# Eight modulation products move from TensorE to VectorE, and the expert ring gets a seventh buffer

## The chip, the cores and the metric

The kernel runs on one core of a Trainium2 chip. The metric is the device time of one execution in microseconds (us). It was measured three times; the median is 1368.77 us. A separate, profiled execution gives the trace that is read below.

## The reference

A two-part transformer block in float32, 256 tokens of width 1024. The change touches the modulation vectors of the first part and the buffers of its experts. Cut to what matters:

```python
# _adaln: one row vector c, silu, times w_mod (1024 x 6144), plus b_mod; six chunks of 1024
sh1, sc1, g1, sh2, sc2, g2 = split(silu(c) @ w_mod + b_mod, 6)
hc = rmsnorm(ctx, norm1_g) * (1 + csc1) + csh1      # csc1, csh1: the same with c_ctx
hx = rmsnorm(x,   norm1_g) * (1 + sc1)  + sh1
# w_in (1024 x 5664) gives u, q, k, v, g, gates and the low-rank decays; for ctx only k, v, decays
ox = gla_bidirectional(qx, kx, vx, ...)             # 4 heads, chunks of 64
x  = x + g1 * mixer_out(pooled, ox, ...)
x  = x + g2 * hier_moe(rmsnorm(x, norm2_g) * (1 + sc2) + sh2, ...)
# hier_moe: 32 experts, each w1, w3 (1024 x 512) and w2 (512 x 1024); top 2 of one group per token
# then two layers (attention + MLP) and four layer norms: second_block
```

w_mod is read as 12 slabs of 1024 x 512. Slabs 0 to 3 (sh1, sc1) are needed at once, for x and for ctx. Slabs 4 to 11 (g1, sh2, sc2, g2) are needed only for x, at the end of the mixer and later.

## The kernel before

**Stages.** The mixer (to about 332 us of the trace), the experts (to about 773 us), two layers (to the end). All weights are read in slabs of 2 MB by DMAs that SP issues in one order (`slab_plan`), each into one of eleven slots of SBUF. The issue waits until the slab that was in the slot before (`BEFORE`) has been used (`slab_freed`). SP works through its queue in order, so a load that waits holds all later ones.

**Each engine's order is written out by hand.** PSUM is used as a ring of four banks; `bank_plan` lists every use in order, with the engine (V or A) that empties it. A use of a bank by TensorE waits until the use four places earlier has been emptied. Behind each other in TensorE's queue in the mixer stand: keys, ctx keys, `v` 0 and 1 (values of x, first half), `cum`, `remc` (decays), `v` 2 and 3 (ctx), `qT`, `v` 4 and 5, `v` 6 and 7, then four heads (`states`, `crossings`, `read_out`), `u`, `g` and the rest of the mixer, which is one long run of matmuls. A w_in slab is split into a high part (ScalarE, `pre_hi`, the tile `prehi`) and a low part (VectorE, `pre_lo`, `prelo`), in two halves, and each `v` or `qT` product waits for the low parts.

**Modulation slabs 4 to 11, before.** `mod_rows(s)` on TensorE multiplies the 32-column tile `scol` (silu of c, 8 tiles of 128 rows) with the slab: eight matmuls, four at a time in four 32-column groups of the array, which leave four partial rows in a bank. ScalarE copies them (`mod_hi`), VectorE takes the rest (`mod_low`, `mod_lo`), and `mod_bc(s)` adds the four rows and spreads the sum to all partitions by two matmuls with the constant `row_pick`. VectorE's `mod_bc(s)` adds the result to the bias rows. All eight slabs but one use slot 2, one after the other. The w_in slabs share the slots 0, 1 and 2 with them. Slot 10 (the tile `own`) is free, and takes slab 2 of the experts early, at the load of modulation slab 6.

**Experts.** Experts are worked on one after the other, four to a turn: an up product (w1 and w3), a down product (w2), and the scatter into the accumulator. Slabs 0 to 10 of the 96 (three for each expert) go into eleven slots (`AHEAD_SLOTS`) as the mixer frees them. Slabs 11 to 95 go around six slots (`MOE_SLOTS`); slot 0 is not used again until the first layer's first slab.

Of the kernel before, what the change touches and what calls it, by code (L numbers as in the profile page):

```python
# [7 lines left out]
P = 128  # L8
D = 1024
KT = D // P  # L10
# [4 lines left out]
NH = 4  # L15
# [95 lines left out]
EXPERTS_PER_TURN = 4  # L111
# [7 lines left out]
MODS = (0, 2, 1, 3)  # L119
MIXER_SLOT = {("mod", 0): 2, ("mod", 2): 1, ("mod", 1): 6, ("mod", 3): 2, ("w_in", 2): 0, ("w_in", 3): 1, ("w_in", 1): 0,  # L120
              ("w_in", 4): 1, ("w_in", 0): 0, ("w_in", 5): 1, ("w_in", 6): 2, ("w_in", 7): 0, ("w_in", 8): 1, ("w_in", 9): 2,
              ("w_in", 10): 0, ("pool_br", 0): 1, ("gla_br", 0): 2, ("gla_br", 1): 0, ("w_o", 0): 1, ("w_o", 1): 2}
# [19 lines left out]
def bank_plan():  # L142
# [7 lines left out]
    order += [("mod_rows", 4, "V"), ("v", 0, "A"), ("v", 1, "A")]  # L150
    order += [("cum", i, "A") for i in range(4)]
    order += [("remc", i, "A") for i in range(4)]
    order += [("mod_bc", 4, "V"), ("mod_rows", 5, "V"), ("v", 2, "A"), ("v", 3, "A"), ("mod_bc", 5, "V"), ("qT", 0, "V"), ("qT", 1, "V")]
    order += [("mod_rows", 6, "V"), ("v", 4, "A"), ("v", 5, "A"), ("mod_bc", 6, "V"), ("mod_rows", 7, "V"), ("v", 6, "A"), ("v", 7, "A")]
    order += [("mod_bc", 7, "V"), ("mod_rows", 8, "V")]
    for h in range(NH + 1):
        if h < NH:
            order += [("s0", h, "A"), ("sT", (h, 0), "V"), ("sT", (h, 1), "V")]
        if h == 0:
            order += [("mod_bc", 8, "V")]  # L160
        else:
            order += [("o", h - 1, "A")] + [("mod_bc", h + 7, "V")] * (h > 1) + [("mod_rows", h + 8, "V")] * (h < NH)
    order += [("u", 0, "A"), ("u", 1, "A")] + [("g", (0, j), "V") for j in range(2)]
# [21 lines left out]
OWN_SLOT = 10  # L185
AHEAD_SLOTS = (3, 6, OWN_SLOT, 1, 5, 2, 4, 7, 8, 0, 9)
MOE_SLOTS = (OWN_SLOT, 3, 6, 5, 1, 2)
# [6 lines left out]
for _n, (_name, _s) in enumerate(SLABS):  # L194

    if _name == "moe":
        _slot = AHEAD_SLOTS[_s] if _s < AHEAD else MOE_SLOTS[(_s - AHEAD) % len(MOE_SLOTS)]
# [44 lines left out]
def build(nc, a, out):  # L242
# [8 lines left out]
    with ctx:  # L251
# [69 lines left out]
        mod_hi, mod_lo = (split_at(f"mod_{what}", 44 * K1 + 512 * i, 512) for i, what in enumerate(("hi", "lo")))  # L321
# [83 lines left out]
        row_pick = ctx.enter_context(nc.sbuf_tensor("row_pick", [P, P], F32R))  # L405
# [67 lines left out]
        names = "x1_ready modhi_ready row_pick_ready tmp_ready base_ready ssq_ready lstd_ready centred_sum ht_ready hid_ready hlow_ready hsq_ready hhi_ready hlo_ready chi_ready clo_ready prehi_ready prelo_ready pre_used kT_done kc_done kT_ready ghi_ready glo_ready yhi_ready ylo_ready mlow_ready gated mixed zhi_ready zlo_ready abs_ready L_ready lr_ones whi_ready split_ready xhi_ready xlo_ready atthi_ready chosen_ready flag_ready pick_ready put_ready dcol_ready dsilu_scaled scol_zero scol_ready square_ready nstd_ready tn_ready mod_ready c_ready exp1_ready lr_part keys_ready cross_ready h_ready ez_ready ostd_ready on_ready z_ready lg_diff rexp_ready comb_ready ssq_half out_stored eps_ready ttok_ready gain_ready s1_ready hidT_ready put_done projected rope_read rot_ready value_ready scored masked max_ready exp_ready turned_done pT_ready weighted_done att_ready share_diff share_exp scaled_ready crossed_done attlo_ready".split()  # L473
# [149 lines left out]
        def slab_freed(n):  # L623
# [10 lines left out]
            if name == "w_in":  # L634
                bank_use = {0: ("u", 1), 1: ("qT", 1), 3: ("v", 3), 4: ("v", 7)}[s]
            else:
                bank_use = ("mod_rows", s)
# [33 lines left out]
        def _(sp):  # L671
# [31 lines left out]
            moe0, per, ring_ = SLAB_AT["moe", 0], 12, len(MOE_SLOTS)  # L703
            looped = AHEAD + ring_
# [4 lines left out]
            for (name, s), n in SLAB_AT.items():  # L709
# [14 lines left out]
                if (name, s) == ("w_in", 9):  # L724
                    load_expert(moe0, 0, 0)
                    spread(bc_n2, a["norm2_g"][0], bc2_in)
                    sp.dma_start(xres, a["x"][0].rearrange("(a p) n -> p a n", p=P)).then_inc(x_again, 16)
                if (name, s) == ("w_o", 1):
# [19 lines left out]
                elif 3 <= s < looped or s >= looped + per * (TURNS - 2):  # L748
                    s = {3: 9, 5: 3, 6: 5, 8: 6, 9: 10, 10: 8, 11: 12, 12: 11}.get(s, s)
# [16 lines left out]
                elif s == looped:  # L766
                    def loads_of_turn(it):
                        for j in range(looped, looped + per):
                            what, before = slab_freed(moe0 + j - ring_)
# [26 lines left out]
        def _(act):  # L796
# [26 lines left out]
            def mod_rows(s):  # L823
                b = take("mod_rows", s)
                if s in MODS:
                    act.activation(mod_slot(s), b, ACT.Copy).then_inc(freed["A"], 1)
                else:
                    act.activation(mod_hi, b, ACT.Copy).then_inc(G["modhi_ready"], 1)
# [93 lines left out]
            mod_rows(4)  # L922
# [12 lines left out]
            mod_rows(5)  # L935
# [5 lines left out]
            mod_rows(6)  # L941
# [3 lines left out]
            mod_rows(7)  # L945
# [4 lines left out]
            mod_rows(8)  # L950
# [7 lines left out]
            for h in range(NH):  # L958
# [5 lines left out]
                if h + 1 < NH:  # L964
                    mod_rows(h + 9)
# [292 lines left out]
        def _(dve):  # L1258
# [52 lines left out]
            def mod_low(s):  # L1311

                b = bank_of("mod_rows", s)
                dve.wait_ge(G["modhi_ready"], s - 3)
# [1452 lines left out]
```

## Time and profile before

| what | value |
|---|---|
| median of 3 runs | 1368.77 us (1365.86 to 1369.69) |
| profiled execution, its own time | 1368.02 us |
| its span in the trace | 1366.2 us |
| TensorE busy | 1198.1 us, 88% of the span |
| VectorE busy | 651.6 us, 48% |
| ScalarE busy | 485.2 us, 36% |
| DMA | 371.95 MB, mean 272 GB/s |
| chain that ended last | PE 69%, DMA 23%, DVE 3%, ACT 2% |

The profile page gives shares over the whole span. This kernel has three stages with different limits, so the windows by stage say more than the page: they give, for a stretch of time, how long each engine was busy, the granted TensorE clock and the DMA rate. The chain that ended last tells what each stretch waited for. The timeline gives single instructions with the idle time before them in square brackets. PE is TensorE, PEld its weight loads, DVE is VectorE, ACT is ScalarE, SPq the queue of SP. An fp32 matmul stands in the trace as two instructions.

### The profile page before, as it was taken

The numbers are of one execution on the slowest core, as the hardware profiler recorded it, in microseconds if no ns is written. First come the engines' busy times: TensorE is split into PE (matmuls) and PEld (weight loads), VectorE is DVE, ScalarE is ACT, GpSimd is POOL, SyncE is SP. The second block draws the span as 40 slices with busy tenths as digits, with TensorE's granted clock in tenths as the row PEclk, the third lists the DMA queues.
The fourth block names the chain that finished last, engine by engine and source line by source line (L and its number), as shares of the span: only waits on it lengthen the run. The fifth ranks groups of instructions, "written<-read, shape, count | busy, mean of one in ns | idle before, by whom it ended". The sixth has DMA issues, their size and how long they took to land.

```text
span 1366.2 us, 22173 instructions
## 1 busy us (share of the span) xinstructions
PE 1198.1 (88%) x9435; PEld 921.6 (67%) x9435; DVE 651.6 (48%) x991; ACT 485.2 (36%) x695; POOL 0.2 (0%) x4
## 2 busy tenths in 40 slices
PE   5999999999866666766766899999999999999997
PEld 4677788887434233433433599878888799888886
DVE  4445446786121010210101377576666767766665
ACT  5552346555101000000000346454444456554443
POOL 0000000000000000000000000000000000000000
PEclk9999999999998887888987999999999999999999
DMA  9677666579999999999999972436364444554620
GB/s 343 257 254 239 223 227 247 198 279 385 412 375 427 427 428 428 426 427 429 428 428 427 397 260 98 150 123 246 134 237 151 175 155 154 185 203 166 223 86 31
DMA packets 89115, 371.95 MB, mean 272 GB/s; under 512 B 6490, under 2 KB 8328, under 8 KB 76364
## 3 DMA queue, kind: packets, MB, share of 16 engines
q1 hardware_dynamic: 87480, 369.73, 69.1%
q10 hardware_dynamic: 1556, 1.08, 0.3%
q8 instruction: 61, 1.00, 0.3%
q14 instruction: 18, 0.15, 0.0%
HBM read 369.74 MB, written 1.05 MB: 271 GB/s over the span
## 4 chain that ended last, share of the span: by engine, by line
PE 69%; DMA 23%; DVE 3%; ACT 2%; issue 1%; SPq 1%; ACTq 0%; DVEq 0%
DMA arena<-in_moe_w 20%; PE ring L2038 8%; PE ring L2482 7%; PE ring L2027 5%; PE acc L2130 4%; PE acc L2131 4%; PE acc L2132 4%; PE ring L2040 4%; PE ring L2029 2%; DMA arena<-in_w_mod 2%; PE acc L2011 2%; PE acc L2013 2%; PE acc L2012 2%; PE ring L2176 1%; PE ring L2178 1%; PE ring L2177 1%
## 5 line engine op out<-in xcount | busy, mean ns | idle before, releaser
L2482 PE MATMUL ring<-arena 128*32 128x256 f32 x2048 | 153.6, 466 | 73.9 <-DMA arena<-in_moe_w 73.9
L2482 PEld LDWEIGHTS ring<-arena 128*32 128x32 f32 x2048 | 76.4, 133 | 146.5 <-DMA arena<-in_moe_w 69.4
L1284 DVE TENSOR_TENSOR wlo<-arena,whi 128x2048 fp32r<-128x2048 f32 x56 | 128.0, 2290 | 49.9 <-ACT whi L843 49.9
L1708 DVE TENSOR_TENSOR arena<-arena,ring 128x128 f32<-128x128 f32 x32 | 12.1, 379 | 257.7 <-ACT arena L1088 257.7
L1088 ACT ACTIVATE arena<-ring 128x128 f32<-128x128 f32 x32 | 8.9, 277 | 349.1 <-PE ring L2482 349.1
L843 ACT ACTIVATE whi<-arena 128x2048 fp32r<-128x2048 f32 x56 | 106.8, 1910 | 42.2 <-PE acc L2132 25.4
L2038 PE MATMUL ring<-xboth,whi 128*128 128x512 f32 x320 | 113.8, 398 | 0.0
L2040 PE MATMUL ring<-xboth,wlo 128*128 128x256 f32 x320 | 89.8, 281 | 0.0
L2038 PEld LDWEIGHTS ring<-xboth,whi 128*128 128x128 f32 x320 | 60.1, 188 | 14.6
L2027 PE MATMUL ring<-hboth,w1hi 128*128 128x512 f32 x192 | 67.4, 395 | 0.1
L2511 PE MATMUL acc<-above 32*128 32x256 f32 x512 | 45.7, 425 | 24.7 <-DVE above L1715 17.9
L2130 PE MATMUL acc<-whi,hidhi 128*128 128x512 f32 x168 | 65.9, 392 | 0.8 <-DVE hidlo L1952 0.8
L2131 PE MATMUL acc<-wlo,hidhi 128*128 128x512 f32 x168 | 65.6, 391 | 0.0
L2132 PE MATMUL acc<-whi,hidlo 128*128 128x512 f32 x168 | 65.4, 389 | 0.0
L2040 PEld LDWEIGHTS ring<-xboth,wlo 128*128 128x128 f32 x320 | 60.4, 189 | 0.7
L1284 DVE TENSOR_TENSOR w3lo<-arena,w3hi 128x2048 fp32r<-128x2048 f32 x22 | 50.4, 2291 | 20.6 <-ACT w3hi L843 20.6
L1239 ACT ACTIVATE arena<-ring 128x256 f32<-128x256 f32 x64 | 24.1, 383 | 95.1 <-PE ring L2040 91.0
L2011 PE MATMUL acc<-xboth,whi 128*128 128x256 f32 x192 | 57.0, 297 | 0.0
L2038 PE MATMUL ring<-xboth,w3hi 128*128 128x512 f32 x160 | 56.9, 398 | 0.0
L2511 PEld LDWEIGHTS acc<-above 32*128 32x128 f32 x512 | 20.3, 183 | 52.6 <-issue 30.6
L1284 DVE TENSOR_TENSOR w1lo<-arena,w1hi 128x2048 fp32r<-128x2048 f32 x21 | 48.1, 2289 | 13.6 <-ACT w1hi L843 13.4
L2013 PE MATMUL acc<-xboth,wlo 128*128 128x256 f32 x192 | 54.3, 283 | 0.0
(420 smaller groups left out, 2648.8 us busy)
## 6 DMA issues: line engine op xcount, KB each, us to landing
arena<-in_moe_w SPq DMA_DIRECT2D x79, 2048.0 KB, 20.5
arena<-in_mlp_w_in SPq DMA_DIRECT2D x16, 2048.0 KB, 9.8
arena<-in_mlp_w_out SPq DMA_DIRECT2D x16, 2048.0 KB, 7.6
own<-in_moe_w SPq DMA_DIRECT2D x15, 2048.0 KB, 24.9
arena<-in_w_mod SPq DMA_DIRECT2D x11, 2048.0 KB, 8.3
arena<-in_w_in SPq DMA_DIRECT2D x11, 2048.0 KB, 9.3
arena<-in_moba_w_qkv SPq DMA_DIRECT2D x6, 2048.0 KB, 19.0
arena<-in_dil_w_qkv SPq DMA_DIRECT2D x4, 2048.0 KB, 8.8
```

The source lines that it names most:

```text
L843: act.activation(hi, raw, ACT.Copy).then_inc(G["whi_ready"], 1)
L1284: dve.tensor_tensor(lo, raw, hi.bitcast(F32), ALU.subtract).then_inc(G["split_ready"], 1)
L2011: pe.matmul(o, whi_, xhi_, start=first, stop=False, skip_group_check=True)
L2013: return pe.matmul(o, wlo_, xhi_, start=False, stop=last, skip_group_check=True)
L2027: pe.matmul(b.rearrange("p (s t) -> p s t", s=2), wh[:, kt, m], both[:, :, kt, :], start=(kt == 0), stop=False, skip_group_check=True)
L2038: pe.matmul(b.rearrange("p (s t) -> p s t", s=2), wh[:, kt, m], xboth[:, :, kt, :], start=(kt == 0), stop=False, skip_group_check=True)
L2040: ins = pe.matmul(b[:, T:2 * T], wl[:, kt, m], xhi[:, kt, :], start=False, stop=(kt == KT - 1), skip_group_check=True)
L2130: pe.matmul(o, hi[:, k0 + k, t_], wh[:, k, c], start=(first and k == 0), stop=False, skip_group_check=True)
L2131: pe.matmul(o, hi[:, k0 + k, t_], wl[:, k, c], start=False, stop=False, skip_group_check=True)
L2132: ins = pe.matmul(o, lo[:, k0 + k, t_], wh[:, k, c], start=False, stop=(last and k == ks - 1), skip_group_check=True)
L2482: ins = pe.matmul(o, xs[:, kt, j, :], w[kt][g], start=(kt == 0), stop=(kt == KT - 1))
L2511: pe.matmul(acc[:, tt, D // 4 * g:D // 4 * (g + 1)], putT[p_, j, tt * P:(tt + 1) * P], ys[p_, :], start=False, stop=True, skip_group_check ...
```

## The change

Modulation slabs 4 to 11 are no longer multiplied on TensorE. `mod_sum(s, first, last)` on VectorE multiplies the tiles `first` to `last` of the slab, 128 x 512 each, with the column of `scol` and sums them into `mod_part`: one tensor_scalar for tile 0 and seven scalar_tensor_tensor for the others, each of which waits for the one before. `mod_bc(s)` on TensorE then is one fp32 matmul with a matrix of ones, which adds the 128 partitions and spreads the sum. `mod_rows`, `mod_hi`, `mod_low` and `row_pick` go for these slabs.

The slabs alternate between slot 2 (even) and slot 10 (odd), and are loaded a little earlier in the order. Expert slab 2 now follows after modulation slab 11 is used, ahead of pool_br. Slabs 11 to 95 of the experts go around seven slots (`TURN_SLOTS`, twelve slabs to a round: slots 0 and 5 once, the others twice). The first layer's slab 0 (slot 0) has to wait for expert slab 90.

```diff
-MIXER_SLOT.update({("mod", s): 1 if s == 9 else 2 for s in range(4, 12)})
+MIXER_SLOT.update({("mod", s): OWN_SLOT if s % 2 else 2 for s in range(4, 12)})
...
-    order = [("mod", 0), ("mod", 2), ("w_in", 2), ("mod", 1), ("mod", 3), ("w_in", 3), ("mod", 4), ("mod", 5), ("w_in", 1), ("mod", 6), ("w_in", 4), ("mod", 7), ("w_in", 0)]
-    order += [("mod", 8), ("mod", 9), ("mod", 10), ("w_in", 5), ("mod", 11)]
+    order = [("mod", 0), ("mod", 2), ("w_in", 2), ("mod", 1), ("mod", 3), ("w_in", 3), ("mod", 4), ("mod", 5), ("w_in", 1), ("mod", 6), ("mod", 7), ("w_in", 4), ("mod", 8), ("w_in", 0)]
+    order += [("mod", 9), ("mod", 10), ("w_in", 5), ("mod", 11)]
...
-MOE_SLOTS = (OWN_SLOT, 3, 6, 5, 1, 2)
+TURN_SLOTS = (3, 6, 5, 1, 2, OWN_SLOT, 0, 3, 6, 1, 2, OWN_SLOT)
...
-                    load_expert(moe0 + 2, 2, 0)
...
+                if (name, s) == ("pool_br", 0):
+                    sp.wait_ge(*slab_freed(SLAB_AT["mod", 11]))
+                    load_expert(moe0 + 2, 2, 0)
...
-                    s = {3: 9, 5: 3, 6: 5, 8: 6, 9: 10, 10: 8, 11: 12, 12: 11}.get(s, s)
+                    s = {3: 9, 5: 3, 6: 5, 8: 6, 9: 10, 10: 8, 11: 12, 12: 13, 13: 11, 17: 18, 18: 17}.get(s, s)
...
+            def mod_sum(s, first, last):
+
+                n = SLAB_AT["mod", s]
+                w, part = view(n, KT, 512), mod_part[:, s % 2, :]
+                for kt in range(first, last):
+                    scale = scol[:, kt, 0:1]
+                    if kt:
+                        dve.wait_ge(G["part_ready"], KT * (s - 4) + kt)
+                        ins = dve.scalar_tensor_tensor(part, w[:, kt, :], scale, part, ALU.mult, ALU.add)
+                    else:
+                        dve.wait_ge(landed[SLOT_OF[n]], 16 * NTH[n])
+                        if s >= 6:
+                            dve.wait_ge(bank_full, BANK_AT["mod_bc", s - 2] + 1)
+                        ins = dve.tensor_scalar(part, w[:, kt, :], scale, None, ALU.mult)
+                    ins.then_inc(G["part_ready"], 1)
...
             def mod_bc(s):
-                moved(pe, "mod_rows", s)
                 b = bank("mod_bc", s)
-                if s == 4:
-                    pe.wait_ge(G["row_pick_ready"], 1)
-                pe.matmul(b, row_pick[:, :], mod_hi, start=True, stop=False)
-                full(pe.matmul(b, row_pick[:, :], mod_lo, start=False, stop=True))
+                pe.wait_ge(G["part_ready"], KT * (s - 3))
+                full(pe.matmul(b, ones, mod_part[:, s % 2, :], start=True, stop=True))
```

In VectorE's queue the sums stand so: slab 4 (tiles 0 to 6) ahead of `pre_lo(3)`, its last tile and slab 5 behind the decays; 6 ahead of `pre_lo(4)`; 7 ahead of `pre_lo(6)`; 8 ahead of `pre_lo(8)`; 9, 10 and 11 in pieces between the heads. TensorE's `mod_bc(11)` moves from before `u` to behind it.

VectorE, around `pre_lo(3)` (`prelo<-arena,prehi` is a low part, L1391 the decays; `mod_lo` is `mod_low`). Before:

```order
L1289 TENSOR_TENSOR prelo_66<-arena,prehi_64 128x2048 [waits prehi_ready]
L1391 TENSOR_TENSOR arena<-arena 128x1024 [waits ez_ready,bank_freed_by_vector]
L1391 TENSOR_TENSOR arena<-arena 128x1024
L1391 TENSOR_TENSOR arena<-arena 128x1024 [waits ez_ready]
L1391 TENSOR_TENSOR arena<-arena 128x1024
L1393 CAST row_pick<-const 128x128 [waits consts_in]
L1315 TENSOR_TENSOR mod_lo<-ring,mod_hi 128x512 [waits modhi_ready]
```

After (L1316 and L1311 are `mod_sum`, L1396 the decays):

```order
L1316 TENSOR_SCALAR above<-arena,above 128x512 [waits slab_landed2,bank_freed_by_vector,scol_ready]
L1311 SCALAR_TENSOR_TENSOR above<-arena,above 128x512 [waits part_ready] x6
L1281 TENSOR_TENSOR prelo_64<-arena,prehi_62 128x2048 [waits prehi_ready]
L1396 TENSOR_TENSOR arena<-arena 128x1024 [waits ez_ready,bank_freed_by_vector]
L1396 TENSOR_TENSOR arena<-arena 128x1024
L1396 TENSOR_TENSOR arena<-arena 128x1024 [waits ez_ready]
L1396 TENSOR_TENSOR arena<-arena 128x1024
L1311 SCALAR_TENSOR_TENSOR above<-arena,above 128x512 [waits part_ready,consts_in]
L1316 TENSOR_SCALAR above<-own,above 128x512 [waits slab_landed10]
L1311 SCALAR_TENSOR_TENSOR above<-own,above 128x512 [waits part_ready] x7
```

Fifteen operations of the sums now stand around the decays, seven of them ahead of the low part.

TensorE, behind `v` 7 at the end of the values (L2294 is `states`, L2308 `crossings` of head 0, L2086 `mod_rows`, L2101 and L2102 `mod_bc`). Before:

```order
L2178 MATMUL ring<-prehi_64,clo 128x512
L2101 MATMUL ring<-mod_hi,row_pick 128x512 [waits bank_freed_by_vector]
L2102 MATMUL ring<-mod_lo,row_pick 128x512
L2086 MATMUL ring<-arena,above 32x512 [waits slab_landed2,bank_freed_by_vector]
L2086 MATMUL ring<-arena,above 32x512 x7
L2294 MATMUL ring<-arena 128x256 [waits bank_freed_by_scalar,keys_ready]
L2294 MATMUL ring<-arena 128x256 x3
```

After (L2112 is `mod_bc`, L2299 `states`, L2313 `crossings`):

```order
L2188 MATMUL ring<-prehi_62,clo 128x512
L2112 MATMUL ring<-above,const 128x512 [waits part_ready,bank_freed_by_scalar]
L2299 MATMUL ring<-arena 128x256 [waits bank_freed_by_vector,keys_ready,bank_freed_by_scalar]
L2299 MATMUL ring<-arena 128x256 x3
L2313 MATMUL ring<-arena 64x64 [waits bank_freed_by_scalar]
L2313 MATMUL ring<-arena 64x64 x9
L2313 MATMUL ring<-arena 64x64 [waits bank_freed_by_scalar]
```

The eight matmuls of `mod_rows` and their waits for a slab are gone, and two matmuls of `mod_bc` have become one.

SP, the issues of expert slabs 12, 11, 13 to 19 (w1, w3, w2 tell the third of an expert, `own` is slot 10). Before:

```order
L697 DMA arena<-in_moe_w1 128x4096 [waits bank_full]
L697 DMA own<-in_moe_w2 128x4096 [waits bank_full]
L697 DMA arena<-in_moe_w3 128x4096 [waits bank_full]
L697 DMA arena<-in_moe_w2 128x4096 [waits bank_full]
L697 DMA arena<-in_moe_w1 128x4096 [waits bank_full]
L697 DMA arena<-in_moe_w3 128x4096 [waits bank_full]
L773 UNCONDITIONAL_BRANCH
L773 ISA
L697 ISA [waits bank_full]
L697 DMA own<-in_moe_w2 128x4096
```

After, slabs 12, 13, 11, 14, 15, 16, 18, 17, 19:

```order
L698 DMA arena<-in_moe_w1 128x4096 [waits bank_full]
L698 DMA arena<-in_moe_w3 128x4096 [waits bank_full]
L698 DMA own<-in_moe_w2 128x4096 [waits bank_full]
L698 DMA arena<-in_moe_w2 128x4096 [waits bank_full]
L698 DMA arena<-in_moe_w1 128x4096 [waits bank_full]
L698 DMA arena<-in_moe_w3 128x4096 [waits bank_full]
L698 DMA arena<-in_moe_w1 128x4096 [waits bank_full]
L698 DMA own<-in_moe_w2 128x4096 [waits bank_full]
L776 UNCONDITIONAL_BRANCH
L776 ISA
L698 ISA [waits bank_full]
```

Slab 18 (w1 of expert 6) goes to slot 0 and is issued one place earlier, ahead of slab 17.

## Rows read from the trace of the kernel before

**Rows 1.** Page, part 2: granted TensorE clock and DMA rate in 40 slices.
```profile
PEclk9999999999998887888987999999999999999999
GB/s 343 257 254 239 223 227 247 198 279 385 412 375 427 427 428 428 426 427 429 428 428 427 397 260 98 150 123 246 134 237 151 175 155 154 185 203 166 223 86 31
```

**Rows 2.** Windows by stage: us; busy us (count) of PE, PEld, DVE, ACT, POOL; clock; DMA share; GB/s.
```profile
60.00:190.00 130.00, 128.11 (x812) 96.73 (x811) 61.71 (x108) 53.26 (x73) 0.00 (x0) 1.00 0.61 214
190.00:332.00 142.00, 140.55 (x789) 120.60 (x787) 102.84 (x142) 81.25 (x108) 0.00 (x0) 1.00 0.74 278
332.00:389.00 57.00, 47.98 (x704) 29.55 (x704) 15.61 (x51) 9.59 (x15) 0.00 (x0) 1.00 0.90 363
389.00:773.00 384.00, 257.76 (x3210) 138.40 (x3210) 52.29 (x148) 22.86 (x48) 0.00 (x0) 0.85 1.01 427
773.00:1366.00 593.00, 580.78 (x3592) 505.21 (x3592) 393.69 (x499) 289.19 (x410) 0.00 (x0) 1.00 0.46 168
```

**Rows 3.** Chain that ended last: start us, us, what; the expert stage.
```profile
388.74 19.00 DMA arena<-in_moe_w
...
739.42 22.41 DMA arena<-in_moe_w
```

**Rows 4.** Same chain: a modulation product, an fp32 product, the w_in load.
```profile
84.59 0.86 PE ring L2257 x2
...
89.35 1.85 PE ring L2086 x16
102.35 9.04 DMA arena<-in_w_in
111.41 1.93 ACT prehi L851
113.36 2.29 DVE prelo L1289
```

**Rows 5.** Timeline of TensorE: start us, us, operation, idle time before it.
```profile
102.16 0.39 PE L2101 MATMUL ring<-mod_hi,row_pick 128*128 128x512 f32 x1
102.39 0.40 PE L2102 MATMUL ring<-mod_lo,row_pick 128*128 128x512 f32 x1
...
116.96 0.47 PE L2176 MATMUL ring<-prehi,hboth 128*128 128x512 f32 x1 [0.81 <-DVE arena L1417]
...
174.90 1.92 PE L2086 MATMUL ring<-arena,above 128*32 128x512 f32 x16 [0.76 <-DMA arena<-in_w_mod]
...
191.66 0.39 PE L2027 MATMUL ring<-hboth,w1hi 128*128 128x512 f32 x1
```

**Rows 6.** Timeline of VectorE: operations like the new ones.
```profile
13.27 1.42 DVE L1330 TENSOR_SCALAR arena<-arena,nstd 128x1024 f32<-128x1024 f32 x2
...
300.10 0.69 DVE L1568 TENSOR_TENSOR arena<-above,arena 128x512 f32<-128x512 f32 x1
300.82 0.69 DVE L1571 TENSOR_TENSOR arena<-arena 128x512 f32<-128x512 f32 x1
...
323.20 1.42 DVE L1606 SCALAR_TENSOR_TENSOR arena<-arena,lrstd 128x512 f32<-128x512 f32 x2
```

**Rows 7.** Timeline of VectorE: waits in the mixer.
```profile
69.20 2.29 DVE L1289 TENSOR_TENSOR prelo<-arena,prehi 128x2048 fp32r<-128x2048 f32 x1 [5.08 <-ACT prehi L851]
...
138.15 2.29 DVE L1289 TENSOR_TENSOR prelo<-arena,prehi 128x2048 fp32r<-128x2048 f32 x1 [8.31 <-ACT prehi L851]
```

**Rows 8.** Timeline of SP: the DMA issues of expert slabs 17 and 18 to 22.
```profile
369.91 0.35 SPq L697 DMA_DIRECT2D own<-in_moe_w  x1
379.43 10.04 SPq L697 DMA_DIRECT2D arena<-in_moe_w  x5
```

**Rows 9.** Windows around the gap between these loads, columns as in rows 2.
```profile
376.00:381.00 5.00, 4.86 (x80) 2.96 (x76) 3.73 (x12) 0.87 (x2) 0.00 (x0) 1.00 0.40 108
382.00:412.00 30.00, 19.85 (x300) 9.83 (x296) 2.98 (x8) 0.55 (x2) 0.00 (x0) 0.89 1.00 427
```

**Rows 10.** A window at the lower clock, columns as in rows 2.
```profile
404.00:410.00 6.00, 2.22 (x24) 1.08 (x28) 0.00 (x0) 0.00 (x0) 0.00 (x0) 0.50 1.02 434
```

More of the change, by code:

```diff
@@ L161, in bank_plan @@
         else:
-            order += [("o", h - 1, "A")] + [("mod_bc", h + 7, "V")] * (h > 1) + [("mod_rows", h + 8, "V")] * (h < NH)
-    order += [("u", 0, "A"), ("u", 1, "A")] + [("g", (0, j), "V") for j in range(2)]
+            order += [("o", h - 1, "A")] + [("mod_bc", h + 7, "V")] * (1 < h < NH)
+    order += [("u", 0, "A"), ("u", 1, "A"), ("mod_bc", 11, "V")] + [("g", (0, j), "V") for j in range(2)]
     order += [("pool", i, "V") for i in range(2)] + [("g", (1, j), "V") for j in range(2)] + [("y1", i, "V") for i in range(2)]
@@ L320, in build @@
         mod_row = at(44 * K1, 2, 512)
-        mod_hi, mod_lo = (split_at(f"mod_{what}", 44 * K1 + 512 * i, 512) for i, what in enumerate(("hi", "lo")))
+        mod_part = mod_row
         ez = [at(o * K1, 4, DK) for o in (40, 34)]
@@ L768, in loads_of_turn @@
                         for j in range(looped, looped + per):
-                            what, before = slab_freed(moe0 + j - ring_)
+                            what, before = slab_freed(BEFORE[moe0 + j])
                             sp.wait_ge(what, it * len(TURN) + before)
@@ L823, in mod_rows @@
             def mod_rows(s):
[L824 to L828, printed above, removed]
+                act.activation(mod_slot(s), take("mod_rows", s), ACT.Copy).then_inc(freed["A"], 1)
             def split_hi(h):
@@ L1419, in _ @@
             pre_lo(7)
-            mod_low(6)
             fw, bw = (factor[:, d, :, :] for d in range(2))
@@ L1456, in _ @@
             mod_bc(6)
+            mod_sum(8, 0, KT)
             pre_lo(8)
-            mod_low(7)
+            mod_bc(7)
             pre_lo(9)
-            mod_bc(7)
-            mod_low(8)
             for h in range(NH):
@@ L1476, in _ @@
                 dve.wait_ge(G["cross_ready"], 2 * h + 2)
-                if h != 1:
-                    mod_bc(8 + max(h - 1, 0))
-                if h:
-                    mod_low(h + 8)
-            mod_bc(11)
+                if h == 0:
+                    mod_bc(8)
+                    mod_sum(9, 0, 6)
+                if h == 1:
+                    mod_sum(9, 6, KT)
+                    mod_sum(10, 0, 4)
+                if h == 2:
+                    mod_sum(10, 4, KT)
+                    mod_bc(9)
+                if h == 3:
+                    mod_sum(11, 0, 5)
+                    mod_bc(10)
+            mod_sum(11, 5, KT)
             dve.wait_ge(G["ostd_ready"], 1)
@@ L1487, in _ @@
             split_lo(0)
+            mod_bc(11)
             split_lo(1)
@@ L2332, in _ @@
                     read_out(h - 1)
-                    if h > 1:
+                    if 1 < h < NH:
                         mod_bc(h + 7)
-                    if h < NH:
-                        mod_rows(h + 8)
             pre_tokens(8, [bank("u", i) for i in range(2)], hhi, hlo)
+            mod_bc(11)
             paired("g", 0, 0, hboth)
```

51 lines of the change are left out of this document (20 added, 31 removed).

## The prediction

> **What bounds the kernel now.** I read the windows by stage first, because the page's shares mix three stages with different limits. In the mixer TensorE is busy 128.1 of 130 us and then 140.6 of 142 us at full clock, VectorE only 61.7 and 102.8 us, and the DMA queues a good half to three quarters of the time [rows 2]. So TensorE sets the pace there, and each product taken off it should shorten the mixer by nearly its own length, as long as nothing else becomes late. The slices of the page and the window from 389 us on say that the experts are bound by the loads: 427 GB/s without a pause, TensorE busy two thirds of the time and partly at the lower clock [rows 1, 2]. The chain of waits agrees, with nothing but expert loads from 388.7 us to the end of that stage [rows 3]. From 773 us TensorE is busy again in 581 of 593 us; the change leaves this stage alone.
>
> Two things follow. In the expert stage only what starts the train of loads sooner, or fills a hole in it, counts. And the mixer sets when that train starts: slots come free by TensorE's work, so a mixer that ends sooner moves the train as a whole.
>
> **TensorE's products.** Each of the eight slabs loses a `mod_rows` of 1.85 us, here 16 matmul instructions [rows 4]: 8 x 1.85 = 14.8 us. `mod_bc` was two products that start 0.23 us apart, about 0.47 us together [rows 5]. It becomes one fp32 product of two instructions, 0.86 us by a like one in the chain [rows 4]: 8 x 0.39 = 3.1 us more. Two waits of TensorE go as well. The 0.76 us at 174.90 was a wait for a modulation slab, which TensorE no longer reads [rows 5]. The 0.81 us at 116.96 was a wait for VectorE's `qT` step, L1417, which is reached earlier relative to the products around it once the slab product between is gone [rows 5]; here I take it as gone, the other end being that it stays. Together -14.8 + 3.1 - 1.6 = -13.3 us.
>
> **The new wait of TensorE.** `mod_rows(6)` stood between `qT` and `v` 4 and covered the split of w_in slab 4. Its load lands 9.04 us after it was released, then ScalarE's high part takes 1.93 us and VectorE's low part 2.29 us [rows 4]. That load waits for a slot that comes free when `v` 3 is done, which by my count is at about 99.2 us after the change; 99.2 + 9.0 + 1.9 + 2.3 = 112.4 us, while TensorE has done `qT` at about 111.5. Behind that wait stand the rest of the values and all heads, so its 1.0 us counts in full. The nearest row of the trace is the 0.81 us wait at the same kind of place [rows 5]; bounds are 0 and about 2 us (the load now shares the queues with modulation slab 7, issued ahead of it). Sum for the mixer: -12.3 us. Laying the queues of the three engines side by side from the order gave -12.0 for the first product of `g`, at 191.66 before [rows 5]; I take **-12.0 us**.
>
> **VectorE's sums.** Each slab adds one tensor_scalar over 512 columns and seven scalar_tensor_tensor, each waiting for the one before. A tensor_scalar over 1024 columns takes 0.71 us (two in 1.42), so one over 512 takes between 0.36 and 0.71; I take 0.45. A scalar_tensor_tensor over 512 with a column as the scalar takes 0.71 (two in 1.42), and two operations on 512 columns of which the second needs the first start 0.72 us apart [rows 6]. So a slab costs 0.45 + 7 x 0.72 = 5.5 us, eight cost 44 us. Against that, eight `mod_low` of 0.69 us, by an operation of that size [rows 6], go: -5.5 us. VectorE's load from 60 to 190 us rises from 61.7 to about 61.7 + 44 - 5.5 = 100 us, of a stretch shortened to 118 [rows 2]. It fits, but no longer loosely: what counts is where the sums stand.
>
> Slab 4's seven tiles, 0.45 + 6 x 0.72 = 4.8 us, stand ahead of `pre_lo(3)`, in a wait of 5.08 us [rows 7]. Slab 8's, 5.5 us, stand in a wait of 8.31 us ahead of `pre_lo(8)` [rows 7], which shrinks but does not close. Slabs 5, 6 and 7 follow in the queue where VectorE has no such hole; by my count slab 6's sum still leaves `pre_lo(4)` 1.3 us before `v` 2 needs it, and slab 7's ends just as ScalarE delivers the high part of w_in slab 4. In the heads VectorE becomes busy about 95% of the time, with 1 to 2 us to spare at each step that TensorE waits for. Cost taken: 0. If the spare time is too short, what stands behind a late sum is a low part or a `cross` of a head, and TensorE waits for either; that is the second rival.
>
> **Queues of SP.** The modulation slabs alternate between two slots, so their loads wait less. Expert slab 2 is loaded later, ahead of pool_br; the queues have room in the mixer (61 to 74% [rows 2]), and it is needed only with the first expert. I cost this at nothing; if its cover were gone, it would be one slab's transfer, 2.1 MB at 427 GB/s [rows 2] = 4.9 us.
>
> **The ring.** With six slots, slab 17 is issued at 369.91 and the next, 18, only at 379.43, since its slot waits for an expert's product [rows 8]. In the window 376 to 381 the queues move 108 GB/s instead of the 427 of the next window [rows 9]: 5 x (1 - 108/427) = 3.7 us of transfer lost, and with a dip of the rate a little earlier I get 4.6 us. After the change slab 18 goes to slot 0, which was freed before that, and is issued ahead of 17. It fills this hole. From about 382 us on the queues have no pause, and the chain runs through them to the end of the stage [rows 3, 9], so what is gained here arrives there. The gain can't be more than one slab's 4.9 us, nor more than what is lost: I take **-4.6 us**, between 3.7 and 4.9, and 0 if slot 0 comes free later than I think. Later in the stage a seventh buffer gives nothing, as the queues are full already. Layer 0's first slab must now wait for a product of expert 30; by my count it is still issued behind loads that keep the queues busy. Cost 0; if it came late, up to one slab, 4.9 us.
>
> **Sum.** The profiled execution took 1368.0 us, 0.8 below the median. 1368.0 - 12.0 - 4.6 = **1351.4 us**, 1352 against the median. Without the removed wait of 0.8, with 2 us of new wait and 3.7 from the ring: 1354.1. Without a new wait and with 4.9 from the ring: 1350.1; and with another 2 us for sizes of the products not in rows, 1348. The likeliest case's own range is 1348 to 1355.
>
> **Rivals.** (1) As above: the mixer's 12 and the ring's 4.6 us both reach the end.
>
> (2) VectorE holds TensorE at a few places. For it: 95% load in the heads, and sums ahead of low parts. Against it: the holes of 5.08 and 8.31 us [rows 7]. Missing the spare time by 1 to 2 us at four places costs 4 to 8 us: 1355.4 to 1359.4.
>
> (3) The ring gives nothing, as another wait of the same expert stands behind it: 1356.0. For it: the experts' products use the slots in the old order. Against it: the hole in the loads [rows 9].
>
> (4) The mixer gain is swallowed before the loads that start the train, which then start when they did: only the ring's 4.6 us are left, 1363.4. Against it: those loads wait for TensorE's work in the mixer, not for a queue (74% busy [rows 2]).
>
> (5) The clock. TensorE stays at full clock, 2.4 GHz, through the mixer despite waits of 0.76 and 0.81 us [rows 2, 5], and falls to half, 1.2 GHz, where the loads hold it for long: busy 2.22 of 6 us [rows 10]. If the new waits together let it fall once or twice, stretches of some 6.6 us at half clock would cost half of that each, 3.3 us: 1354.7 to 1358.0. The Trainium skill, page TensorE: Matmul & The Clock Gate, section HAM oscillation, tells of this: waits for data between bursts of matmuls let the clock fall again and again, and each costs. By that rule a kernel with more short waits would be slower; the trace agrees in the expert stage and not for waits under 1 us in the mixer.
>
> (6) Slower than before: VectorE becomes the bound of the mixer. The 64 operations of the sums would each have to take x us more than the 0.69 us of mean I count. VectorE's load of 100 us reaches the shortened stretch's 118 and eats the 16.6 us of gain if 100 + 64 x = 118 + 16.6, so x = 0.54: from about 1.2 us per operation on. If each took double, 1.4 us, that is 100 + 44 - 118 = 26 us more against 16.6 gained: 1377. Against it: the like operations run at 0.69 to 0.72 us [rows 6].
>
> **How the numbers follow.** Chances: (1) 0.67, (2) 0.14, (3) 0.08, (4) 0.03, (5) 0.05, (6) 0.03. About 0.3%, 4.1 us, is what a measurement can tell from no change. All cases but (6) and the far edge of (4) are faster by more: faster 0.93, same 0.03, slower 0.04. The range runs from 1347, just below the likeliest case's end, to 1360, and takes in (2), (3) and (5).
>
> **What the profile after would show.** The slab products of 16 instructions appear only for slabs 0 to 3; `g` starts at about 179.7 us (191.66 before, L2027 [rows 5]); TensorE waits about 1 us for the low part ahead of `v` 4; the sums' operations start 0.72 us apart; no window near 370 us has a rate far below 427 GB/s; the experts end at about 756 us; the last stage is still 593 us. I would be wrong if TensorE's waits in the heads name a `cross` or low part of VectorE with more than 2 us in all, if the sums step at over 1 us, or if the loads of the experts show the same hole one slab later.

## The result, and the profile after

The changed kernel takes 1349.41 us in the median of 4 runs (1347.14 to 1350.68), the kernel before 1367.55 us (4 runs). The ratio is 0.9863, with a 95% interval from 0.9849 to 0.9877: 18.1 us less, between 17 and 21 us. The forecast was 1351.4. The profiled execution after took 1348.45 us, its span is 1346.4 us against 1366.2.

The page of the changed kernel, part 2, granted TensorE clock and DMA rate in 40 slices:

```profile
PEclk9999999999998878888887999999999999999999
GB/s 341 330 201 278 221 280 241 225 316 381 422 425 428 428 428 427 426 428 428 428 428 425 307 250 142 172 102 211 198 178 203 127 157 173 172 228 147 236 77 32
```

They have the shape of [rows 1]: a clock at or near full and a varying rate in the mixer, then some 427 GB/s to the end of the experts. The windows by stage, with the columns of [rows 2]:

```profile
60.00:178.00 118.00, 117.34 (x697) 95.86 (x696) 100.99 (x163) 51.45 (x66) 0.00 (x0) 1.00 0.61 209
178.00:320.00 142.00, 140.27 (x802) 121.05 (x802) 105.11 (x154) 81.52 (x110) 0.00 (x0) 1.00 0.79 301
320.00:377.00 57.00, 47.40 (x718) 27.97 (x720) 14.14 (x40) 7.21 (x12) 0.00 (x0) 1.00 0.97 399
377.00:755.00 378.00, 253.05 (x3186) 137.80 (x3182) 53.46 (x149) 24.71 (x52) 0.00 (x0) 0.86 1.01 426
755.00:1346.00 591.00, 579.77 (x3586) 504.43 (x3584) 391.78 (x496) 287.40 (x406) 0.00 (x0) 1.00 0.46 168
```

In the first window VectorE is busy 101.0 of 118 us, where it was 61.7 of 130, and TensorE 117.3 of 118. In the heads alone VectorE is busy 28.2 of 32 us, 88%:

```profile
135.00:167.00 32.00, 32.00 (x271) 26.08 (x270) 28.20 (x61) 10.56 (x25) 0.00 (x0) 1.00 0.65 228
```

The third window, the first experts, moves 399 GB/s where it moved 363. The other stages are as in [rows 2].

To share out the 19.8 us between the two spans, four places serve that both kernels have: where the products of the values begin (in the kernel before, `mod_rows(4)` ahead of them), the first product of the pooling (`const,arena`, 16 instructions), the gather of the first expert turn (`ttok` with `pick`, 32 instructions), and the first product of the layers (`acc<-xboth`). TensorE in the kernel before (timeline; the second row is from the chain):

```profile
67.09 1.92 PE L2086 MATMUL ring<-arena,above 128*32 128x512 f32 x16
...
197.47 1.78 PE ring L2345 x16
...
332.29 3.81 PE L2468 MATMUL ring<-arena 128*128 128x128 f32 x32 [0.38 <-issue]
...
777.36 2.87 PE L2057 MATMUL acc<-xboth,whi 128*128 128x256 f32 x22 [0.82 <-ACT xboth L1114]
```

And after, where the values begin at 67.16 us:

```profile
182.96 1.78 PE ring L2349 x16
...
317.24 3.81 PE L2472 MATMUL ring<-arena 128*128 128x128 f32 x32 [0.37 <-issue]
...
757.49 4.07 PE L2070 MATMUL acc<-xboth,whi 128*128 128x256 f32 x32 [0.83 <-ACT xboth L1106]
```

| stretch | before | after | difference |
|---|---|---|---|
| start to the values | 67.1 | 67.2 | +0.1 |
| values and heads, to the pooling | 130.4 | 115.8 | -14.6 |
| rest of the mixer, to the first gather | 134.8 | 134.3 | -0.5 |
| experts | 445.1 | 440.3 | -4.8 |
| layers, to the end of the span | 588.8 | 588.9 | +0.1 |

So both gains that were forecast reach the end, the mixer's 14.6 (12.0 forecast) and the ring's 4.8 (4.6 forecast).

**The one wait left in the values and heads.** TensorE's timeline after, ahead of `v` 4, and around `mod_bc(8)`:

```profile
111.71 0.47 PE L2186 MATMUL ring<-prehi,hboth 128*128 128x512 f32 x1 [0.66 <-DVE prelo L1281]
...
138.76 1.13 PE L2112 MATMUL ring<-above,const 128*128 128x512 f32 x2
139.72 1.89 PE L2299 MATMUL ring<-arena 128*128 128x256 f32 x8
```

TensorE waits 0.66 us for the low part, L1281. The load is not what holds it. ScalarE's high part of w_in slab 4:

```profile
106.71 1.92 ACT L850 ACTIVATE prehi<-arena 128x2048 fp32r<-128x2048 f32 x1 [5.58 <-DMA arena<-in_w_in]
```

The slab landed at 106.7 us, some 8.0 us after `v` 3 had released its slot at 98.7 (9.04 in [rows 4]), and the high part is there at 108.6. The chain that ended last goes another way:

```profile
99.23 1.92 ACT prehi L850
101.20 2.17 issue
103.38 0.49 DVE above L1316
103.89 0.76 DVE above L1311
...
108.62 0.75 DVE above L1311
109.37 2.21 DVE prelo L1281
```

It goes through VectorE's sum of slab 7 (L1316 and L1311), whose last operation ends at 109.37, and only then does the low part start. VectorE's own queue is the releaser. The rows show too that an operation of the sum starts 0.79 us after the one before (the second at 103.89, the eighth at 108.62), not 0.72.

**The ring.** SP's issues of slab 18 and of slab 17 after it:

```profile
351.51 0.33 SPq L698 DMA_DIRECT2D arena<-in_moe_w  x1
354.68 0.33 SPq L698 DMA_DIRECT2D own<-in_moe_w  x1
```

A window of the changed kernel at the place where [rows 9] had its hole, 15 us earlier on the clock of the trace:

```profile
361.00:366.00 5.00, 4.87 (x84) 2.93 (x80) 3.67 (x12) 0.88 (x2) 0.00 (x0) 1.00 1.08 423
```

It moves 423 GB/s where there were 108.

### The profile page after: what moved, and what is told of

Read it like the earlier page. It is cut to its first block, busy times and chain, and to the rows that moved or that the text cites. A ratio compares the mean times of both kernels' runs of the same rounds, so it can differ in the third digit from the quotient of the medians.

```text
span 1346.4 us, 21986 instructions
## 1 busy us (share of the span) xinstructions
PE 1181.2 (88%) x9307; PEld 918.5 (68%) x9307; DVE 690.8 (51%) x1046; ACT 481.2 (36%) x687; POOL 0.2 (0%) x4
## 4 chain that ended last, share of the span: by engine, by line
PE 70%; DMA 22%; DVE 3%; ACT 2%; issue 2%; SPq 1%; ACTq 0%; DVEq 0%
DMA arena<-in_moe_w 20%; PE ring L2051 8%; PE ring L2486 7%; PE ring L2040 5%; PE acc L2140 4%; PE acc L2141 4%; PE acc L2142 4%; PE ring L2053 4%; PE ring L2042 2%; PE acc L2024 2%; PE acc L2025 2%; PE acc L2026 2%; PE ring L2186 1%; PE ring L2188 1%; PE ring L2187 1%
## 5 line engine op out<-in xcount | busy, mean ns | idle before, releaser
L2486 PE MATMUL ring<-arena 128*32 128x256 f32 x2048 | 150.2, 458 | 72.8 <-DMA arena<-in_moe_w 72.8
L2051 PEld LDWEIGHTS ring<-xboth,whi 128*128 128x128 f32 x320 | 60.1, 188 | 14.6
L2515 PE MATMUL acc<-above 32*128 32x256 f32 x512 | 45.7, 425 | 24.8 <-DVE above L1728 18.1
L2024 PE MATMUL acc<-xboth,whi 128*128 128x256 f32 x192 | 57.0, 297 | 0.0
L2025 PE MATMUL acc<-xboth,whi 128*128 128x256 f32 x192 | 54.3, 283 | 0.0
```

Source lines behind the costliest of these rows:

```text
L2024: pe.matmul(o, whi_, xhi_, start=first, stop=False, skip_group_check=True)
L2025: pe.matmul(o, whi_, xlo_, start=False, stop=False, skip_group_check=True)
L2051: pe.matmul(b.rearrange("p (s t) -> p s t", s=2), wh[:, kt, m], xboth[:, :, kt, :], start=(kt == 0), stop=False, skip_group_check=True)
L2486: ins = pe.matmul(o, xs[:, kt, j, :], w[kt][g], start=(kt == 0), stop=(kt == KT - 1))
```

## The experiments

Each time is the median of 4 to 10 runs. Stretches are measured between the places of the table above, in the profiled execution of each kernel: "the values and heads" stands for the second, "the experts" for the fourth. They show less scatter than the whole time. The same kernel's whole time varies by some 5 us (1366.07 to 1370.97 for the kernel before, in 13 runs), and the profiles show where most of that comes from: TensorE's granted clock. Windows from 40 to 50 us, where TensorE has the same work in all twelve kernels, of the kernel before, the ring alone, the loads' order alone and the changed kernel:

```profile
40.00:50.00 10.00, 10.00 (x96) 6.92 (x92) 4.31 (x10) 4.57 (x7) 0.00 (x0) 0.83 0.98 363
40.00:50.00 10.00, 10.00 (x68) 7.24 (x64) 4.31 (x10) 4.57 (x7) 0.00 (x0) 0.66 0.96 341
40.00:50.00 10.00, 10.00 (x102) 6.90 (x99) 5.14 (x12) 5.33 (x9) 0.00 (x0) 1.00 1.03 358
40.00:50.00 10.00, 10.00 (x96) 6.85 (x92) 4.31 (x10) 4.57 (x7) 0.00 (x0) 0.83 1.01 361
```

The clock falls to 0.50 there in nine of the twelve profiles. What is lost is (1 - clock) x 10 us: nothing in three profiles, 1.7 us in seven, 3.4 us in two. The values begin at 65.5 to 65.7, at 67.1 to 67.3 and at 68.8 us, in just these groups, and the groups don't follow the edits. The rest of the mixer takes 134.3 to 135.0 us in nine profiles. In the three others (135.5 with the ring alone, 135.7 with the sums alone, 137.1 with the halved products) the clock falls once more, between 311 and 332 us, in a piece of code that no edit touches.

### The ring alone, and the sums alone

The first is the kernel before with `TURN_SLOTS` and its order of issues, the second the changed kernel with the six slots and the order of before. No other line differs.

> The kernel before with the seven-slot ring alone (and its order of issues), the modulation products still on TensorE. Theory (the two parts are separate, the ring fills the hole of the loads near 376 us): 4.8 us less than before, about 1363. Rival (the hole is filled only because the mixer ends sooner, or the ring gives nothing by itself): within 1 us of before. The traces of before and after give -19.9 us at the end of the experts and -15.05 at their start, so the ring's part there is 4.8.

Measured: 1365.58 us, ratio to before 0.9977 (0.9963 to 0.9991), 1 to 5 us less. In the time this is about 2 us, less than the 4.8 expected; the stretch decides. The experts take 440.7 us against 445.1: 4.4 less. The values and heads take 130.5, as before. In the profiled execution the values begin 1.7 us later than in the kernel before, at 68.8, by the clock, which hides a part in its span.

> The changed kernel with the six-slot ring of before. Theory: it keeps the 15.0 us of the mixer and gives back the ring's 4.8, about 1353.5 to 1354. Rival (the parts interact: with a shorter mixer the hole moves or grows): it differs from the changed kernel by 0 or by more than 6 us.

Measured: 1354.48 us, 5.1 more than the changed kernel. The values and heads take 115.8 us, exactly as there, and the experts 445.3, as before. So the two parts add up: 14.6 and 4.4 to 4.8 us.

### The order of slabs 17 and 18

```diff
-                    s = {3: 9, 5: 3, 6: 5, 8: 6, 9: 10, 10: 8, 11: 12, 12: 13, 13: 11, 17: 18, 18: 17}.get(s, s)
+                    s = {3: 9, 5: 3, 6: 5, 8: 6, 9: 10, 10: 8, 11: 12, 12: 13, 13: 11}.get(s, s)
```

> The changed kernel, but expert slabs 17 and 18 issued in their own order. My prediction counted on 18 going ahead of 17. In the trace after, slab 16 lands only at 358.4 us and 17 and 18 could be issued at 354.7 and right behind, so the queues stay busy either way. Theory now: no difference (within 0.5 us of the changed kernel). Rival (the place of 18 in the order fills the hole): 3 to 5 us slower than the changed kernel.

Measured: 1352.10 us, 2.7 more than the changed kernel. The values begin 1.6 us late in this profile, by the clock; the experts take 441.9 us against 440.3, so the place of slab 18 is worth 1.6 of the ring's 4.8 us (the seven other kernels with seven slots take 440.0 to 440.7 us there). My expectation of no difference was wrong, and the rival's 3 to 5 us was too much. SP's issues here, slab 17 and then 18 and the next two:

```profile
356.94 0.33 SPq L698 DMA_DIRECT2D own<-in_moe_w  x1
357.31 10.18 SPq L698 DMA_DIRECT2D arena<-in_moe_w  x3
```

And a window with its rate:

```profile
367.00:373.00 6.00, 5.08 (x80) 2.60 (x82) 1.87 (x5) 0.60 (x1) 0.00 (x0) 1.00 0.93 337
```

Slab 17 waits until 356.94 us, 18 and the rest queue behind it, while slab 16 is moved until 360.2. In the changed kernel 18 is issued 3.2 us ahead of 17, and 6.9 us before slab 16 lands there (358.4). Here the window after the two has 337 GB/s instead of 427, so the loss is in the loads again. Its cause is only argued: 18 is in the queue just 2.9 us before slab 16 lands, but the low rate comes 10 us later, behind the issue of the next two loads at about 367 us.

### What a product costs

```diff
-                for half in range(2):
+                for half in range(2 if s in MODS else 1):
...
-                        ins = pe.matmul(b[32 * g:32 * g + 32, :], scol[:, kt, :], w[:, kt, :], start=(half == 0), stop=(half == 1))
+                        ins = pe.matmul(b[32 * g:32 * g + 32, :], scol[:, kt, :], w[:, kt, :], start=(half == 0), stop=(half == 1 or s not in MODS))
```

> The kernel before, with half of each modulation product of slabs 4 to 11 left out (four of the eight matmuls, so only half of the rows are multiplied); loads, waits and the rest as before. Theory (a product costs TensorE its own time, 1.9 us): half of it, 0.95 us, goes 8 times, 7.6 us less, and perhaps 0.5 us more or less by waits: 1359.5 to 1360.5. Rival (most of the gain came from the loads' new order and from waits, not from the products): less than 4 us.

Measured: 1361.85 us, ratio 0.9952 (0.9936 to 0.9969), 6.0 us less, 1.4 us above the expected range. The profiled execution is the slowest of the four, 1367.23 us against 1359.99 to 1361.86 of the others, so what follows holds for this one. The values and heads take 127.2 us, only 3.1 less. TensorE's waits in that stretch (waits view: who waited for what, us in total, times, longest):

```profile
PE ring L2086 <- DMA arena<-in_w_mod: 2.1, 1, 2.1
PE ring L2308 <- DVE arena L1323: 1.2, 1, 1.2
PE ring L2176 <- DVE arena L1417: 0.7, 1, 0.7
```

The wait for a modulation slab has grown from 0.76 to 2.14 us and the one of `crossings` (L2308) from 0.32 to 1.18. And something else shows behind the wait for the slab. Windows of this kernel, columns as in [rows 2]:

```profile
168.00:171.00 3.00, 0.89 (x4) 0.40 (x3) 0.69 (x1) 0.60 (x1) 0.00 (x0) 1.00 0.17 63
171.00:172.00 1.00, 0.97 (x8) 0.19 (x8) 0.00 (x0) 0.00 (x0) 0.00 (x0) 1.00 0.00 0
172.00:173.00 1.00, 1.00 (x7) 0.80 (x4) 0.22 (x1) 0.85 (x3) 0.00 (x0) 0.57 0.00 0
173.00:174.00 1.00, 1.00 (x4) 0.82 (x3) 0.47 (x1) 0.65 (x4) 0.00 (x0) 0.50 0.77 74
174.00:175.00 1.00, 1.00 (x4) 0.82 (x3) 0.00 (x0) 0.00 (x0) 0.00 (x0) 0.50 0.74 240
175.00:176.00 1.00, 1.00 (x5) 0.77 (x5) 0.00 (x0) 0.00 (x0) 0.00 (x0) 0.72 1.05 399
```

TensorE is busy throughout after 171, but from about 172.1 to 175.6 at half the clock. The read-outs behind the short product take 5.06 us (171.03 to 177.08, less the product's 0.99) where they took 3.37 (174.90 to 180.13, less 1.86): 1.7 us lost to the clock. So 3.1 + 1.4 + 0.9 - 0.15 (a wait that shrank from 0.81 to 0.66) + 1.7 = 6.9 us, 8 x 0.87. Half a product is 0.87 us, and the trace has 0.99 us for the half that is left (171.03 to 172.02), together about the 1.85 of a whole one. So its price is TensorE's own time. The expectation's 0.95 for a half was too much.

The rest of the mixer takes 2.3 us longer in this profile as well, by a second fall of the clock:

```profile
322.00:330.00 8.00, 8.00 (x22) 4.42 (x21) 4.83 (x24) 6.50 (x9) 0.00 (x0) 0.57 0.94 356
```

No wait of TensorE above 0.4 us stands ahead of it from 180 us on.

### What the new product costs

```diff
+                pe.matmul(b, ones, mod_part[:, s % 2, :], start=True, stop=True)
```

> The changed kernel with each mod_bc matmul of slabs 4 to 11 issued twice. Theory (the fp32 product costs TensorE 0.86 us, as I priced it): 8 x 0.86 = 6.9 us more than the changed kernel. Rival (it costs 0.46 us, the distance at which the trace shows the next product starting behind it): 3.7 us more.

Measured: 1352.44 us, 3.0 more. The values and heads, however, take 121.7 us against 115.8: 5.9 more, and TensorE waits nowhere in them, so the 0.66 us are covered as well. (5.9 + 0.66) / 8 = 0.82 us for each product, near the 0.86 of [rows 4]. The whole time shows less, because in this profile the values began at 65.65 us, 1.5 us earlier, with no fall of the clock ahead of them. That is the scatter that the stretches avoid. The trace's distance of 0.46 us to a following product says nothing on the cost. It stands ahead of a product with high or low parts (122.72 to 123.18 in the changed kernel), and the one behind that then starts 0.63 us later instead of 0.23. In the rows above `mod_bc(8)` starts at 138.76 and `states` only at 139.72.

### How near VectorE is to being the bound

```diff
...
+                        for i in range(4):
+                            dve.tensor_scalar(part, w[:, kt, :], scale, None, ALU.mult).then_inc(G["pad_done"], 1)
+                            dve.wait_ge(G["pad_done"], 4 * (s - 4) + i + 1)
```

The first of the two runs has a 1 in the place of each 4. `pad_done` is a new semaphore; its name is added to the list of names.

> The changed kernel with one further tensor_scalar of 128x512 at the head of each of the eight sums (the first tile's product done twice), 8 x 0.51 = 4.1 us more on VectorE, which was busy 101 of 118 us. Theory (the places matter, not the total: sums 6, 7 and 10 have next to no room, the others some): TensorE waits 0.5 us longer at v 4 and up to 1 us more elsewhere, 0.5 to 2 us more. Rival A (VectorE has room in all): 0. Rival B (VectorE is the bound in the heads): 4 us more.

Measured: 1350.36 us, 0.9 more. The values and heads take 117.2 us, 1.4 more for 4.1 us of further work.

> As the last, with four further tensor_scalars for each sum, 8 x 2.04 = 16.3 us more on VectorE, about all of its idle time of 17 us. Theory (the room is in the wrong places): 8 to 14 us more than the changed kernel. Rival (only the total counts): 0 to 3 us more. It puts a row on the case in which VectorE becomes the bound, which I had from 0.54 us more per operation (35 us in all) on.

Measured: 1355.56 us, 6.2 more. The values and heads take 124.0 us, 8.2 more for 16.3 us of further work. The expected 8 to 14 us are met by the stretch, at their low end, and not by the time; the values begin 1.7 us earlier in this profile, at 65.5, where the clock did not fall. TensorE's waits, and the stretch as a window:

```profile
PE ring L2189 <- DVE prelo L1281: 2.2, 2, 1.3
PE ring L2027 <- DVE prelo L1281: 2.1, 1, 2.1
PE ring L2302 <- DVE arena L1479: 2.0, 1, 2.0
PE ring L2327 <- DVE above L1328: 1.4, 1, 1.4
PE ring L2316 <- DVE arena L1479: 0.3, 1, 0.3
```

```profile
65.00:190.00 125.00, 117.00 (x693) 94.63 (x692) 112.27 (x186) 46.57 (x64) 0.00 (x0) 1.00 0.60 205
```

The waits, 8.0 us, are all for VectorE: low parts, `cross` (L1479) and `mod_bc` (L1328), yet VectorE is busy only 112.3 of 125 us. So the place of the work decides, not its sum, and about a third to a half of what is added arrives at the end. The clock stayed at 1.00 in spite of a wait of 2.09 and one of 1.95 us.

### The wait ahead of `v` 4

```diff
-            mod_sum(7, 0, KT)
+            mod_sum(7, 0, 6)
...
+            mod_sum(7, 6, KT)
             pre_lo(7)
```

> The changed kernel, with the last two tiles of slab 7's sum moved behind pre_lo(6) and the qT step on VectorE. In the trace after, TensorE waits 0.66 us ahead of v 4 for pre_lo(6), which starts when the sum of slab 7 ends (109.36 us), 0.7 us after ScalarE's high part is there. Theory (VectorE's queue holds it): the wait vanishes, 0.6 us less, about 1348.8. Rival (the load of w_in slab 4 holds it, as I predicted): the wait stays at 0.6 us or more.

Measured: 1349.65 us, no difference in time. The wait ahead of `v` 4 is gone, but a smaller one for the next low part has come:

```profile
PE ring L2187 <- DVE prelo L1281: 0.3, 1, 0.3
```

The values and heads take 115.6 us, 0.2 less. That the load holds TensorE is refuted. A second try puts the two tiles one place further back:

```diff
-            mod_sum(7, 0, KT)
+            mod_sum(7, 0, 6)
...
             pre_lo(7)
+            mod_sum(7, 6, KT)
```

> The changed kernel with the last two tiles of slab 7's sum behind pre_lo(7) instead of ahead of pre_lo(6). In the run with them between qT's step and pre_lo(7) the wait ahead of v 4 went, and 0.27 us of a wait for pre_lo(7) took its place, so v's stretch was 0.22 us shorter. Theory (VectorE's queue is all that holds TensorE there): no wait of TensorE above 0.15 us from mod_bc(4) to g, that stretch 0.6 us shorter than in the changed kernel, the time 1348.8, which can't be told from 1349.4. Rival: a wait of another cause shows in its place.

Measured: 1347.89 us (1347.09 to 1348.27), ratio to before 0.9848 (0.9832 to 0.9865). Against the changed kernel's 1349.41 this is 1.5 less, with ranges that overlap; the profile supports 0.7 of it. The values and heads take 115.1 us, and no wait of TensorE is listed in them. It has the lowest median of this study.

### The loads' order alone

The kernel before with the change's `MIXER_SLOT` for slabs 4 to 11, its order in `slab_plan` and the later load of expert slab 2. The products stay on TensorE.

> The kernel before with the change's load order and slots for modulation slabs 4 to 11 (slots 2 and 10 in turn, expert slab 2 later), but the products still on TensorE and the six-slot ring. Theory (the products' own time is the gain; of the mixer's 14.9 us between mod_rows(4) and g only the 0.76 us wait for a slab hangs on the loads): that wait goes, 0.5 to 1 us less in that stretch than before, which a time can hardly tell from 1367.6. Rival (the loads' order brings a good part of the gain): 4 us less or more.

Measured: 1368.12 us, ratio 0.9999 (0.9989 to 1.0010). The values and heads take 129.6 us against 130.4: 0.8 less, the wait for the slab at 174.90, which is no longer listed. In the time it can't be seen.

## Why the prediction was right, and where it was off

**Which case came.** The first rival, both gains, at -19.8 us in the profile where -16.6 were forecast. Rival (3), that the ring gives nothing, fell with the ring alone, and rival (4) with the table of stretches: what the mixer gains is there at the end of the experts. The errors that follow nearly all lie on one side, 3.2 us in the profile. That the median came within 2.0 us of the forecast is partly luck: the profiled execution of the changed kernel lies 1.0 us below its median, the one of the kernel before 0.5 above.

**The products, 14.8 us.** The unit of 1.85 us holds: leaving out half of one saves 0.87 us. The loads' order alone brings 0.8 us, so it is not what shortens the mixer.

**`mod_bc`, +3.1 us: too much.** The new product's 0.86 us is confirmed (0.82 by doubling it). The old pair was underestimated. I took 0.47 us from the one place where it stands between products of its own kind [rows 5]. TensorE in the kernel before, at `mod_bc(6)` and at the crossings of head 0:

```profile
127.95 0.39 PE L2101 MATMUL ring<-mod_hi,row_pick 128*128 128x512 f32 x1
128.19 0.40 PE L2102 MATMUL ring<-mod_lo,row_pick 128*128 128x512 f32 x1
128.51 0.64 PE L2086 MATMUL ring<-arena,above 128*32 128x512 f32 x4
...
146.96 0.92 PE L2308 MATMUL ring<-arena 128*64 128x64 f32 x20 [0.32 <-DVE arena L1323]
```

Ahead of a slab product, as at `mod_bc(6)`, the pair takes 0.56 us to the start of the next (127.95 to 128.51). Behind the read-outs it takes 0.65 and 0.75 us by its starts (180.13 to 180.78, 163.95 to 164.70), but there it starts some 0.2 us before the read-out's step of 0.86 us is over, which leaves 0.46 and 0.56. Over eight pairs that is an estimate of about 4.3 us instead of 3.8, so the exchange costs +2.6, not +3.1.

**The waits, -1.6: too little.** The last row above is a wait that I had left out. The crossings of head 0 took 2.09 us from 145.72 to 147.81, with a listed wait of 0.32, while they take 1.48 in the changed kernel (137.28 to 138.76). With these 0.61 us the removed waits are 0.81 + 0.76 + 0.61 = 2.2 us.

**The new wait, +1.0.** It is 0.66 us, and my cause was wrong. I had the load as the last to come, with the high part done at 110.1 us and the low part at 112.4. The high part was done at 108.6: the load took 1.1 us less than in [rows 4], and its slot came free at 98.7, not 99.2. The sum of slab 7 did not end "just as ScalarE delivers" but 0.7 us later, at 109.4. Its own length explains 0.5 us of that: 5.99 us instead of 5.5, because I priced an operation at 0.72 us and it steps at 0.79. The experiments on the order of slab 7's sum show that it was the sum that held TensorE: with it out of the way the wait vanishes.

These terms give -14.8 + 2.6 - 2.2 + 0.7 = -13.7 against 14.6 measured. The remaining 0.9 us stay unexplained. A candidate is the step from one kind of product to another, which the forecast left out: behind a slab product the second product with high or low parts starts 0.33 us after the first (91.14 to 91.47 in the kernel before), not 0.23. The 0.5 us in the rest of the mixer are within its scatter between kernels; one piece of it ran at a slower pace in the kernel before, as the last section tells.

**VectorE's sums.** Predicted 5.5 us for a slab and 100 us of load. A slab measured 6.0 us (103.38 to 109.37), and the load 101.0. The cost of 0 was right but for the wait at `v` 4. In the heads VectorE is busy 88% of the time, not 95. That it has some room there holds, since TensorE never waits for it, but not at every step the 1 to 2 us that I gave: with 0.51 us more per sum TensorE waited once in the heads (0.87 us at 159.2), with 2.04 us more three times.

**The ring, -4.6 us.** Measured -4.8 and, alone, -4.4. The mechanism was right, and so was the place of slab 18 ahead of 17, though I doubted it after I had seen the trace. The experiment gives it 1.6 us; the free slot alone gives the other 3.1. One reading was wrong: [rows 3] are not followed by "nothing but expert loads". From 525 to 562 us the chain of the kernel before goes over the experts' own products and a piece without a listed wait:

```profile
537.85 5.14 issue
```

The loads run on at 426 GB/s meanwhile, and the gain arrived all the same.

**The rival of the clock.** From the values to the pooling it did not come in the changed kernel: no wait of TensorE there exceeds 0.66 us, and the clock is 1.00. That TensorE "stays at full clock through the mixer" is wrong for its start, though: [rows 2] begin at 60 us, and between 42 and 46 us the clock fell in the kernel before as in the changed one, 1.7 us each, so the difference is free of it. With the halved products it fell behind a wait of 2.14 us for a slab, TensorE ran at half clock for about 3.5 us, and 1.7 us were lost. The Trainium skill, page TensorE: Matmul & The Clock Gate, section HAM oscillation, tells of falls behind waits for data; its own case has waits of about 3 to 5 us. No run here ties the fall to the wait: 2.09 and 1.95 us left the clock at 1.00 in another kernel, and at 311 to 332 us it fell in three profiles and not in nine, with no such wait ahead.

**The slower side** was not reached: 16.3 us of further work on VectorE cost 8.2 of the 19.4 us gained. If each microsecond beyond that arrived in full, 16.3 + 11.2 = 27.5 us would use up the gain; if it arrived at the same half, some 38 us. Both are estimates, and the forecast's 35 us lies between them.

## What to carry to other kernels

Work taken off the engine that is busy all the time shortened the stretch by its full length here, because the engine that took it over did so at places with room. What decides is the gap ahead of the operations that are waited for, not the sum of the busy time. Measure the price of an operation that is removed at every kind of neighbour it has, not at one. A further ring buffer was worth the one hole that it filled, and a third of that hung on the order of the issues. Before you compare two profiles by their spans, look at the granted clock in the parts that no edit touches: here it alone moved the start of the values by up to 3.4 us.

## What was not expected of the hardware

- A chain of scalar_tensor_tensor over 128x512 float32, with a column as the scalar, steps at 0.79 us, while a tensor_tensor of the size that waits for the one before steps at 0.72 [rows 6], and the first, a tensor_scalar, at 0.51 us (103.38 to 103.89).
- TensorE's matmul stream has two paces at the same granted clock of 1.00. The same product in the rest of the mixer, in the changed kernel and in the one with two tiles of slab 7's sum behind `pre_lo(7)` (busy us, mean ns):

```profile
L2040 PE MATMUL ring<-gboth,w1hi 128*128 128x512 f32 x64 | 22.2, 394 | 0.0
```

```profile
L2041 PE MATMUL ring<-gboth,w1hi 128*128 128x512 f32 x64 | 22.7, 399 | 0.0
```

394 ns against 399, a per cent. The kernel before has the slower pace too, the loads' order alone the faster one, so it doesn't follow the edits; its cause is open.
- TensorE's clock fell to half in some executions and not in others at the same place of the same code: at 41 to 49 us in nine of twelve profiles, at 311 to 332 us in three of twelve. Each fall lost 1.7 or 3.4 us, counted as (1 - clock) x time. It fell behind one wait of 2.14 us, and not behind waits of 2.09 and 1.95 us in another kernel.
